# Latent attention and RWKV-7 interleaved on half of PSUM each, with the rope arithmetic on GpSimd

## What is computed

```
h = rms_norm(x, attn_norm[l]);  p = h @ w_in[l]
hq, hf, hi, hg, mq, mkv, mkr, rw = split_cols(p, IN_SIZES)
o_hg  = hgrn2_mixer(hq, hf, hi, hg, ...)            # 4 heads of 128
o_mla = mla_mixer(mq, mkv, mkr, cos, sin, ...)      # 8 heads, latent attention
o_rw, v_first = rwkv7_mixer(rw, ...)                # 8 heads of 64
x = x + concat([o_hg, o_mla, o_rw]) @ w_o[l];  x = x + swiglu(rms_norm(x))

mla:  q = rms_norm(q_a) @ w_qb        -> (256, 8, 128+64);  kv = rms_norm(kv_a) @ w_kvb -> (256, 8, 128+128)
      normalise q_nope, q_rope, k_nope, k_rope;  rotate q_rope, k_rope by cos/sin (rope)
      p = softmax(causal(q_nope k_nope^T + q_rope k_rope^T));  o = p v
rwkv: token shift, w = sigmoid/decay, a, g by low-rank products, kk normalised, v mixed with v_first (layer 1)
      state_t = state_{t-1} * w_t + (state_{t-1} . -kk_t) (kk_t a_t)^T + v_t k_t^T;   y_t = state_t r_t
      out = (group_norm(y) + bonus) * g
```

## Time and profile before

| | us |
|---|---|
| median of 3 runs | 2605.68 |
| lowest and highest | 2599.29 and 2606.17 |
| the profiled execution, its own time | 2604.1 |
| its span, first to last instruction | 2602.2 |
| mean granted TensorE clock | 0.963 |
| PE busy | 2475.8 (95%), 14004 matmul records |
| DVE busy | 1361.4 (52%) |
| ACT busy | 1073.2 (41%) |
| POOL busy | 30.6 (1%), of which ten `rw_level` steps |

### The profile page before, as it was taken

The page is one execution under the profiler, slowest core; times in us unless marked ns, Lnnn a source line. Parts: engine busy times, 40 slices in busy tenths (PEclk is TensorE's granted clock), DMA queues, the critical chain, the costliest instruction groups (busy, mean ns, idle before and its releaser), DMA issues.

```text
span 2602.2 us, 33961 instructions
## 1 busy us (share of the span) xinstructions
PE 2475.8 (95%) x14004; PEld 2008.9 (77%) x14004; DVE 1361.4 (52%) x1376; ACT 1073.2 (41%) x1241; POOL 30.6 (1%) x26
## 2 busy tenths in 40 slices
PE   7999868999999999999999997679999999999999
PEld 6888457788888888888888864577888888888887
DVE  5684364654444444445557734546544445444444
ACT  4553341444444434444445533314444434344433
POOL 0000001000000000000000000010000000000000
PEclk9999769999999999999999996799999999999999
DMA  7443300455555555545553431004455555555554
GB/s 289 152 180 122 105 1 3 162 214 193 178 184 186 194 193 179 189 181 189 183 189 143 170 121 65 1 3 177 179 185 186 179 192 188 191 187 181 190 181 142
DMA packets 59999, 411.69 MB, mean 158 GB/s; under 512 B 6608, under 2 KB 6608, under 8 KB 13168
## 3 DMA queue, kind: packets, MB, share of 16 engines
q1 hardware_dynamic: 58624, 401.63, 43.4%
q0 software_dynamic: 1264, 8.43, 0.9%
HBM read 407.94 MB, written 2.10 MB: 158 GB/s over the span
## 4 chain that ended last, share of the span: by engine, by line
PE 92%; DVE 6%; ACT 1%; issue 1%; DMA 0%; DVEq 0%; POOL 0%; POOLq 0%
PE psum L1305 26%; PE psum L1307 26%; PE psum L1306 26%; PE psum L1438 2%; PE psum L1552 2%; PE psum L1633 1%; PE psum L1467 1%; PE psum L1468 1%; PE psum L1357 1%; PE psum L1694 1%; PE psum L1316 1%; DVE arena L1069 0%; DVE arena L1134 0%; DMA gain<-gains_dram 0%; DVE w_lo L739 0%
## 5 line engine op out<-in xcount | busy, mean ns | idle before, releaser
L739 DVE TENSOR_TENSOR w_lo<-raw,w_hi 128x1024 fp32r<-128x1024 f32 (+2 forms) x752 | 902.4, 1205 | 907.1 <-ACT w_hi L374 900.4
L374 ACT ACTIVATE w_hi<-raw 128x1024 fp32r<-128x1024 f32 (+2 forms) x752 | 782.9, 1045 | 1148.4 <-PE psum L1307 1144.6
L1305 PE MATMUL psum<-w_hi,hT_hi 128*128 128x512 f32 (+2 forms) x2112 | 830.4, 393 | 17.2 <-DVE w_lo L739 12.5
L1307 PE MATMUL psum<-w_hi,hT_lo 128*128 128x512 f32 (+2 forms) x2112 | 825.1, 391 | 0.0
L1306 PE MATMUL psum<-w_lo,hT_hi 128*128 128x512 f32 (+2 forms) x2112 | 825.1, 391 | 0.0
L1305 PEld LDWEIGHTS psum<-w_hi,hT_hi 128*128 128x128 f32 x2112 | 399.1, 189 | 107.4 <-issue 12.9
L1307 PEld LDWEIGHTS psum<-w_hi,hT_lo 128*128 128x128 f32 x2112 | 398.9, 189 | 90.9
L1306 PEld LDWEIGHTS psum<-w_lo,hT_hi 128*128 128x128 f32 x2112 | 399.3, 189 | 88.8
L1305 PE MATMUL psum<-w_hi,act_hi 128*128 128x512 f32 x896 | 349.7, 390 | 0.0
L1307 PE MATMUL psum<-w_hi,act_lo 128*128 128x512 f32 x896 | 348.7, 389 | 0.0
L1306 PE MATMUL psum<-w_lo,act_hi 128*128 128x512 f32 x896 | 348.6, 389 | 0.0
(11 more groups left out here) (293 smaller groups left out, 1265.6 us busy)
## 6 DMA issues: line engine op xcount, KB each, us to landing
raw<-stream_dram SPq DMA_DIRECT2D x360, 1024.0 KB, 4.8
raw<-stream_dram SPq DMA_DIRECT2D x16, 512.0 KB, 3.6
raw<-stream_dram SPq DMA_DIRECT2D x8, 768.0 KB, 4.1
raw<-stream_dram SPq DMA_DIRECT2D x8, 640.0 KB, 3.8
gain<-gains_dram POOLq DMA_DIRECT2D x4, 1024.0 KB, 5.7
x<-x_in_dram SPq DMA_DIRECT2D x4, 512.0 KB, 8.2
out_dram<-x SPq DMA_DIRECT2D x4, 512.0 KB, 7.0
lor<-lora_dram POOLq DMA_DIRECT2D x2, 832.0 KB, 13.6
```

Of the source, the lines that this page charges most:

```text
L374: nc.scalar.activation(w_hi[:, q % HALF_RING, 0:2 * w], raw[:, j % 4, hf * 2 * w:(hf + 1) * 2 * w], ACT.Copy).then_inc(hi_done, 1)
L739: tt(w_lo[:, q % HALF_RING, 0:2 * w], raw[:, j % 4, hf * 2 * w:(hf + 1) * 2 * w], w_hi[:, q % HALF_RING, 0:2 * w].bitcast(F32), SUB).then_ ...
L1305: mm(o, a_hi, w_hi[:, r, cols], start=(k == 0), stop=False)
L1307: last = mm(o, a_lo, w_hi[:, r, cols], start=False, stop=(k == n_k - 1))
```

## The change

It interleaves the two mixers, and moves tensors so that both can be under way.

- **PSUM.** The attention now uses banks 4 to 7 for all it does, RWKV-7 banks 0 to 3. The eight up-projections go to banks 4 and 5, 6 and 7 in turn, and each waits for ACT's copy of the second one before it. The second `attend` waits until DVE has read the scores of the first (`mla_s_read`), and so on.
- **SBUF.** `hT_hi` and `hT_lo` are placed in front of the weight rings, and `arena` lies over both, so it grows from 22528 to 30720 columns. RWKV-7's tensors lie in what are the quarters of `hT` that the mixers' results go to only later; `small` gets a sibling `srw`; the buffers of `rw_level` shrink from two to one, in `gain`, as does `v_st`.
- **Rope.** Its eighteen steps move from DVE to POOL, in the same chain of waits. ACT's first stacked copy waits for its end, since `v_st` takes its place in `gain`.
- **Orders.** PE, ACT and DVE get lists in which pieces of both mixers alternate.
- **RWKV-7.** Token shift in four pieces (2, 4, 4 and 4 of the 14 blocks of 128 columns) instead of two; the three products of 128 columns become four of 64, `ar` is gone; the gate's product with `g2` is no longer made in the stage and copied twice by ACT: PE makes it beside the turns of `yc` in the second slot of the output projection, into banks 6 and 7, which DVE reads.
- **Waits.** `plain_used` and PE's wait for itself are gone: SP waits for `mla_up_mm`. The load of the next `gain` by POOL moves from the end of rope to the end of the scan.

The core of the diff (functions and lists by name; where a list is new, it is given as it stands now):

```diff
-        hT_hi = sb("hT_hi", [P, KT, SEQ], F32R)
-        hT_lo = sb("hT_lo", [P, KT, SEQ], F32R)
...
         with ExitStack() as on:
+            hT_hi = sb("hT_hi", [P, KT, SEQ], F32R, on)
+            hT_lo = sb("hT_lo", [P, KT, SEQ], F32R, on)
...
-        ARENA = 22528
+        ARENA = 30720
...
-                        sp.wait_ge(plain_used, N_PLAIN * l + j - N_IN - 3)
+                        sp.wait_ge(S("mla_up_mm"), N_PLAIN * l + j - N_IN - 3)
...
-                pool.wait_ge(S("mla_rope_done"), l + 1)
+                pool.wait_ge(S("mla_up_ready"), 8 * l + 4)
+                pool.wait_ge(S("mla_q_rstd"), l + 1)
+                for t in range(TT):
...
+                    v(tt(rb4[:, t, 0:8, :], q4[:, t, :, NOPE:QK], along(small[:, 48 + 8 * t:56 + 8 * t], ROPE), ALU.mult))
+                    v(tt(rb[:, t, 0:576], rb[:, t, 0:576], row[:, 128:704], ALU.mult))
+                    u(tt(ro4[:, t, 0:9, 0:32], x1, co_, ALU.mult))
+                    u(tt(rtmp[:, t, :, :], x2, si_, ALU.mult))
+                    u(tt(ro4[:, t, 0:9, 32:64], x2, co_, ALU.mult))
+                    settle()
+                    v(tt(ro4[:, t, 0:9, 0:32], ro4[:, t, 0:9, 0:32], rtmp[:, t, :, :], ALU.subtract))
+                    v(tt(rtmp[:, t, :, :], x1, si_, ALU.mult))
+                    v(tt(ro4[:, t, 0:9, 32:64], ro4[:, t, 0:9, 32:64], rtmp[:, t, :, :], ALU.add))
+                    v(nc.gpsimd.tensor_copy(ro4[:, t, 9, :], ro4[:, t, 8, :]))
+                pool.sem_inc(S("mla_rope_done"), 1)
+                pool.wait_ge(S("rw_m_ready"), 5 * l + 1)
+                for k in range(len(RW_LEVELS)):
+                    if k:
+                        pool.wait_ge(S("rw_gt_mm"), 10 * l + 2 * k)
...
+                pool.wait_ge(S("rw_y_mm"), l + 1)
                 pool.dma_start(gain[:, :], gains[2 * l + 1:2 * l + 2, :].broadcast_to([P, D])).then_inc(gain_in, 16)
```

ACT, from the attention's key norms on (`stacked` copies a stacking product out, `gt_out` the product of a level):

```diff
+                up_out(7)
+                q_out(0)
+                k_std(1)
+                act.wait_ge(S("mla_rope_done"), ev)
+                stacked(0, v_st, 0)
+                q_out(1)
+                k_out(0)
...
+                stacked(1, b_st, 2)
+                k_out(1)
+                act.wait_ge(S("mla_s_mm"), 8 * ev)
+                stacked(2, k_st, 0)
+                softmax(0)
+                softmax(1)
+                gt_out(0)
+                probs_out(0)
+                probs_out(1)
+                gt_out(1)
+                mix_out(0)
+                mix_out(1)
```

DVE, from the bonus on, and from the first product on:

```diff
+                vs(tt(rw_a, rw_a, rw_e_b, MUL), "rw_b_done", ev)
+                vs(tt(rw_k, rw_k, rw_e_b, MUL), "rw_k_done", ev)
+                k_norm(0)
+                k_var(1)
+                v(tt(rw_r, rw_r, rw_e_r, MUL))
+                vs(tt(rw_kk, rw_kk, rw_e_kk, MUL), "rw_ab_done", ev)
+                k_norm(1)
...
+                product(1, mab, 2, "strict_lo")
+                score_max(0)
+                product(2, mab_t, 0, "strict_up")
+                v(tt(inv_t, mab_t, over(C("pair_up"), JC, RC), MUL))
+                v(stt(inv_t, inv_t, -1.0, over(idst, JC, RC), MUL, ADD))
...
+                score_max(1)
+                probs(0)
+                level(0)
+                probs(1)
+                level(1)
+                mix_lo(0)
+                mix_lo(1)
+                level(2)
```

PE, from the fifth up-projection on (v1 and v2 are in layer 1 alone):

```diff
+                up(4)
...
+                up(5)
+                pe.wait_ge(S("rw_kk_scale"), ev)
...
+                up(6)
+                pe.wait_ge(S("rw_rk"), ev)
...
+                up(7)
+                q_turn(0)
+                pe.wait_ge(S("rw_kk_normed"), ev)
+                pe.wait_ge(S("rw_v_ready"), ev)
+                stack(rw_v, 0)
+                q_turn(1)
+                k_turn(0)
+                pe.wait_ge(S("rw_b_done"), ev)
+                stack(rw_a, 2)
+                r_turn()
+                k_turn(1)
+                pe.wait_ge(S("rw_k_done"), ev)
+                pe.wait_ge(S("rw_stacked"), 3 * l + 1)
+                stack(rw_k, 0)
+                attend(0)
+                pe.wait_ge(S("rw_ab_done"), ev)
+                pe.wait_ge(S("rw_stacked"), 3 * l + 2)
+                product(rw_kk, rw_a, 2)
+                attend(1)
+                pe.wait_ge(S("rw_stacked"), 3 * ev)
+                product(rw_a, rw_kk, 0)
+                level_g(0)
+                p_turn(0)
+                level_x(0)
+                p_turn(1)
+                level_g(1)
+                mix(0)
+                level_x(1)
+                mix(1)
+                level_g(2)
+                level_x(2)
...
+                            for i in range(4):
+                                mm(bank(6, 2)[:, i * SEQ:(i + 1) * SEQ], lora_of("g2")[:, i * P:(i + 1) * P], pm[:, 13, :],
+                                   start=True, stop=True)
```

More of the change, by code:

```diff
@@ L208, in build @@
[L208 to L219, removed]
@@ L548, in _, with q_std, k_std @@
-                for hf in range(2):
+                def q_std():
+                    act.wait_ge(S("mla_var"), 3 * l + 1)
+                    nc.scalar.activation(small[:, 80:112], small[:, 32:64], ACT.Sqrt).then_inc(S("mla_std"), 1)
+                def k_std(hf):
+                    act.wait_ge(S("mla_var"), 3 * l + hf + 2)
+                    nc.scalar.activation(small[:, 112 + 8 * hf:120 + 8 * hf], small[:, 64 + 8 * hf:72 + 8 * hf],
+                                         ACT.Sqrt).then_inc(S("mla_std"), 1)
@@ new lines, in _ @@
+                nc.scalar.activation(rkT, bank(4)[:, 0:SEQ], ACT.Copy).then_inc(S("mla_rT_ready"), 1)
+                stacked(1, b_st, 2)
[10 more added lines that the diff above has]
+                mix_out(1)
+                for k in range(2, len(RW_LEVELS)):
+                    gt_out(k)
@@ L644, in _ @@
                         act.wait_ge(S("rw_y_var"), ev)
[L645 removed]
+                        nc.scalar.activation(srw[:, 112:128], srw[:, 96:112], ACT.Sqrt).then_inc(S("rw_y_std"), 1)
                     if j == 3:
@@ L1042, in _, with probs @@
                     dve.sem_inc(S("mla_max"), 1)
-                for hf in range(2):
+                def probs(hf):
                     h4 = slice(4 * hf, 4 * hf + 4)
@@ L1143, in _, with product, level @@
-                for k in range(len(RW_LEVELS)):
+                def product(k, dst, b0, mask):
+                    dve.wait_ge(S("rw_m_mm"), 5 * l + k)
+                    vs(tt(dst, bank(b0, 2).rearrange("p (n t) -> p n t", n=JC), over(C(mask), JC, RC), MUL),
+                       "rw_m_ready", 5 * l + k)
+                def level(k):
                     last = k == len(RW_LEVELS) - 1
@@ new lines, in _ @@
+                lora(2, lora_of("wa"), ODD)
+                up(3)
+                pe.wait_ge(S("rw_kk_squares"), ev)
+                pe.wait_ge(S("rw_w_ready"), 4 * ev)
+                for t in range(TT):
+                    for j in range(4):
+                        n = 4 * t + j
+                        last = mm(bank(0)[:, 2 * n:2 * n + 2], rw_tmp[:, j, t * P:(t + 1) * P], C("ones2")[:, 0:P:64],
+                                  start=True, stop=True)
+                last.then_inc(S("rw_kk_mm"), 1)
@@ new lines, in _ @@
+                for j in range(4):
+                    last = mm(bank(2, 2)[:, j * SEQ:(j + 1) * SEQ], rkb[:, j, :], rw_tmp[:, j, :], start=True, stop=True)
+                last.then_inc(S("rw_bonus_mm"), 1)
+                up(7)
[7 more added lines that the diff above has]
+                stack(rw_a, 2)
```

683 lines of the change are left out of this document (337 added, 346 removed).

## The result

| | before | after |
|---|---|---|
| median of 4 runs, us | 2605.51 | 2510.57 |
| lowest and highest | 2599.29 and 2606.17 | 2505.75 and 2511.67 |
| profiled execution, own time and span | 2604.1 and 2602.2 | 2511.67 and 2509.5 |
| stage of layer 0, layer 1 | 208.9, 226.2 | 185.2, 192.3 |
| all the rest of the span | 2167.1 | 2132.0 |

The ratio is 0.9637, with a 95% interval of 0.9618 to 0.9657: 95 us less. I had forecast 49 less, 2557, and a range that ended at 2516. The last two lines of the table say where the mistake is. The stages became 57.6 us shorter, against a forecast of 51.5. The rest, which I had as 4 us longer, is 35 us shorter. It holds nothing but the split products and what runs beside them.

What follows compares the result with a forecast made beforehand. PE, 92% of the chain, bounds the kernel; only its stages' waits and low clock would change. Stages of 187.8 and 195.8 give 383.6 for 435.1, −51.5, plus 4.0 for `g2`: 2604.1 − 47.5, 2557; range 2516 to 2594.

Steps and rivals of the forecast that it cites:

- PE's five waits behind the first scores: Layer 0, second scores to second turns of probabilities: PE waits of 3.2, 1.2, 4.0, 5.2 and 3.7 us.
- 133.2 + 7.6 + 17.7: PE's work in layer 0's stage: 133.2 us of pieces, 7.6 surcharge for low clock, 17.7 busy in the unchanged end.
- 20.9 + 8.4: PE's waits in layer 0's stage: 20.9 us ahead of the scan in the new order, 8.4 in the unchanged end.
- The scores at half clock: Both `attend` in each layer's stage cost 15.0 us apiece, the only duration in the trace, 30.0 together.
- rival A: Scores run at 2.4 GHz, an `attend` taking 8.2 us, 6.8 less; four make −27, total 2526; chance 0.23.
- PE's thin feed: Argument against full clock in the scores: turns and small products lie ahead, as at the low clock from 351 to 390.
- Rope on POOL at nothing: Rope moved to POOL ends at 53 us, ACT asks at about 54; covered by up-projections and first turns, cost nothing.
- rival B: POOL and DVE hold each other up during rope, which ends 12.5 us later than ACT asks: +25, 2582; chance 0.26.
- my sum for POOL: Rope on POOL: 6.6 us for 2880 columns plus 1.8 for perhaps 0.2 between steps, 8.4 a half, 16.8 in all.
- `hT` beside the weight rings … touch no wait of PE: New place of `hT` and later load of `gain` touch no wait of PE; no cost was put on them.
- outside the stage PE does split products that the change does not touch: Only PE's time between its first up-projection and the output projection was taken to count.
- The `g2` products: In the output projection, 8 records of 256 columns that nothing hides: +2.0 us a layer, +4.0 in all.

Runs made afterwards that it cites:

- s_read_first: The changed kernel, but DVE reads the first scores before it masks product 1, the maxima behind the mask: 2484.74 us, ratio to before 0.9549.
- s_rope_dve: The changed kernel with rope's eighteen steps back on DVE, right behind the queries' norm: 2514.04 us, ratio to before 0.9653.
- p_pad64: The kernel before, hT where it was, with 64 bytes per partition left free ahead of the weight rings: 2564.5 us, one execution.
- p_next: The kernel before with hT_hi and hT_lo allocated directly ahead of the weight rings, nothing else changed: 2568.15 us, ratio 0.9866.
- s_pad192: The changed kernel with 192 bytes per partition left free between hT_lo and the weight rings: 2545.68 us, ratio to before 0.9782.

## Why the prediction was wrong

**The stage was nearly right.** 187.8 and 195.8 forecast, 185.2 and 192.3 measured; with the placement taken out, the time is 2545.7 for my 2556.6, 11 us less. PE's five waits behind the first scores came out within 0.1 us of the lists and row durations in layer 0. In part the sum came out by two misses that cancel: PE worked 151.0 us in layer 0, where my terms give 158.5 (133.2 + 7.6 + 17.7), and waited 34.2, where they give 29.3 (20.9 + 8.4). (The listed terms of PE's work add up to 133.0, not 133.2.) The two misses:

- *The scores at half clock*, 15.0 each, "the only duration that the trace has for them". The first in each layer took 8.35 (rival A for that half), the second 14.8 and, in layer 1, where the clock fell 1.5 us after they had begun, 13.5. As s_read_first shows, what decides for the second is the wait right in front, 3.28 us. The first have none in front now; before, PE had waited 3.5 us ahead of the turns in front of them and 1.39 more ahead of the scores. I had weighed PE's thin feed against it, and that was no reason: the feed is the same in s_read_first.
- *Rope on POOL at nothing.* The forecast put its cost in its end, with 1 us to spare, and rival B at +12.5 a layer by the same road. Its mechanism is there, POOL and DVE hold each other up, but it reaches PE by DVE. Ahead of the bonus DVE's steps took 3.6 us more than in s_rope_dve (3.98 for 1.38, and twice 1.70 for 1.23), and PE waited. ACT's first stacked copy began at 304.98, behind a step that had waited for DVE's `k_var` until 304.86; rope had ended at 304.22, so it did not wait for rope. By s_rope_dve the move is worth some 1.8 us a layer, of DVE's 9.0. (The 0.2 us between steps in my sum for POOL stands in no row; the trace has 0.08.)

The Trainium skill (SBUF — State Buffer, "SBUF: two separate sides") has an exclusive lock, for a whole instruction, between a GpSimd operation that reads SBUF and a DVE operation with two SBUF inputs, and between GpSimd and DVE in a two-port performance mode. These traces agree: 3.05 for 1.04, 3.25 for 1.23, and no stretching of the DVE steps that read PSUM. DVE's scalar steps, which read one tensor from SBUF, were stretched too (3.98 for 1.38); no run here shows in which mode they ran. The traces add a size: DVE's loss over a rope of 23 us was 6, not all 13.4 of its steps.

**The step that failed** is one clause: "`hT` beside the weight rings … touch no wait of PE". That is true, and I took it for a cost of nothing. It changes no wait, but the pace of 5952 products that I had set aside with "outside the stage PE does split products that the change does not touch". p_pad64 shows it with 64 bytes and nothing else: −39 us in its one execution, and p_next −35.4 in four. Since the chain is 92% PE, 2.7% of these products weighs as much as two thirds of the whole interleaving (39 us against 59.6). The change without it (s_pad192) takes 35.1 us more than with it, and by the count it is 38. The `g2` products, +4.0 in the forecast, cost 3.5.

What stays open is why the address counts. The rings lie 105,216 bytes behind hT in p_pad64 and 32,768 in p_next; both are at 226.9 ns or under, and modulo 512 they differ, so 256 is enough as a period. The shape between its five points is not fixed, those at 128 and 224 rest on one kernel and one execution each, if on some 5800 starts in its trace, and a single product was never measured by itself. Loads of stationary tiles run beside the products, for 879.4 of the 1053.7 us between the two stages of the changed kernel, so two reads of SBUF at once are the place where I would look, but no run here shows that the cause is there.

## What to carry to other kernels

When a diff moves a tensor that the dominant instruction reads, compare that instruction's mean by operand before costing the move at nothing: 399 against 390 ns of the same shape, in two rows, was worth 39 us. When two mixers are interleaved, order DVE's list by what PE asks for next; a wait of 3.3 us cost 3.3 and then 6.5 again through the clock. And work moved to GpSimd was not free for VectorE here while both read SBUF. Before a difference of 3 us is put down to an edit, compare the granted clock outside the part that was edited.

## What the runs showed that I had not expected

The start-to-start time of a 512-column f32r product is 226.8 ns when the stationary and the moving tensor start at the same address modulo 256 bytes, and up to 233.3 when not. With 256 columns equal addresses are the slow case: 119.8 ns in the changed kernel and 113.6 before (190 starts in each trace). It is not simply the reverse, though: 64 bytes apart it is 114.5, but 128 apart 119.6 and 224 apart 118.4, slow for both widths. And a wait of 3.28 us on PE was enough for the clock to fall, after 8.35 us of scores at full pace, in both layers, while in s_read_first it stayed up over one of 1.11 and fell with the next, of 4.00. Behind the one of 2.48 us in the output projections of the changed kernel it fell in layer 0 and not in layer 1.
